# One decoder step on one core: mLSTM prompt tiles cut into chunk quarters, conv tails, a weight pair and token products moved

## What is computed

```
h = rmsnorm(x, norm_mix);  parts = split(h @ w_in)
h_a = mlstm_chunked(q, k, v, i, log_f, C0, n0, m0)      # chunks of 64 tokens, 4 heads of 128
h_b = gated_delta_chunked(conv(g_qkv), g, beta, S0)     # chunks of 64; conv over 4 tokens
h_c = memory_attention(x_q, mem_k, mem_v)               # 256 memory rows; 8 caches for the samples
mixed = sigmoid(gate_a)*(h_a @ w_a) + sigmoid(gate_b)*(h_b @ w_b) + sigmoid(gate_c)*(h_c @ w_c)
x = x + mixed @ w_out
x = x + hier_moe(rmsnorm(x, norm_ffn))                  # 16 experts of 512, best 2 of the best group
```

## Time and profile before

| what | value |
|---|---|
| median of three runs | 776.87 us (774.41 to 777.2) |
| the profiled execution | 773.82 us, its span 771.7 us, mean granted PE clock 0.98 |
| PE busy | 716.7 us (93%), 4393 records |
| DVE / ACT / POOL busy | 274.6 / 164.5 / 62.3 us |
| chain that ended last, by engine | PE 74%, DMA 15%, DVE 5%, ACT 2%, issue 2% |
| HBM | 174.43 MB read, 16.83 MB written |

### The profile page before, as it was taken

One profiled execution on the slowest core, in us unless ns is written; L12 is line 12 of the kernel. 1 busy time (PEld: TensorE's weight loads), 2 busy tenths in 40 slices (PEclk: granted clock), 3 DMA queues, 4 the chain that ended last, 5 costly groups with the idle time before them and its releaser, 6 DMA issues.

```text
span 771.7 us, 10609 instructions
## 1 busy us (share of the span) xinstructions
PE 716.7 (93%) x4393; PEld 422.0 (55%) x4393; DVE 274.6 (36%) x732; ACT 164.5 (21%) x377; POOL 62.3 (8%) x93
## 2 busy tenths in 40 slices
PE   6999999999989999999999999999999877878784
PEld 3544457877656777777777775543333323323331
DVE  1242013566763761464154352250232101100245
ACT  3221212222455411321131211231010000000014
POOL 3010200010330100000010020020000000001110
PEclk9999999999999999999999999999999989999998
DMA  9983700661399502023325487677999999999991
GB/s 271 343 284 109 192 27 1 236 252 72 96 393 371 187 6 106 1 84 138 109 73 214 138 278 315 243 314 259 391 424 427 407 429 430 411 425 398 431 358 64
DMA packets 49471, 187.25 MB, mean 243 GB/s; under 512 B 5240, under 2 KB 5485, under 8 KB 45322
## 3 DMA queue, kind: packets, MB, share of 16 engines
q1 hardware_dynamic: 40032, 155.52, 52.1%
q0 software_dynamic: 9280, 30.96, 12.1%
q10 hardware_dynamic: 106, 0.03, 0.0%
HBM read 174.43 MB, written 16.83 MB: 248 GB/s over the span
## 4 chain that ended last, share of the span: by engine, by line
PE 74%; DMA 15%; DVE 5%; ACT 2%; issue 2%; SPq 1%; POOL 1%; ACTq 0%; DVEq 0%
PE PS L664 13%; PE PS L1011 12%; DMA arena<-in_w_exp_down 9%; PE PS L1428 8%; PE PS L1023 6%; PE PS L1458 6%; PE PS L753 5%; DMA ring<-in_w_exp_down 3%; PE PS L675 2%; PE PS L780 2%; DMA out_C_s<-ring 2%; PE PS L650 2%; PE PS L1310 2%; PE PS L739 1%; SPq L1533 1%
## 5 line engine op out<-in xcount | busy, mean ns | idle before, releaser
L1428 PE MATMUL PS<-ring,arena 128*64 128x512 f32 x416 | 98.5, 629 | 13.7 <-issue 13.7
L1011 PE MATMUL PS<-hT,ring 128*128 128x288 f32 x384 | 102.2, 414 | 0.0
L1762 ACT ACTIVATE arena<-PS 128x512 f32<-128x512 f32 (+7 forms) x128 | 51.0, 422 | 183.5 <-PE PS L664 51.3
L1011 PEld LDWEIGHTS PS<-hT,ring 128*128 128x128 f32 x384 | 70.1, 190 | 19.6 <-issue 1.5
L1428 PEld LDWEIGHTS PS<-ring,arena 128*64 128x64 f32 x416 | 34.6, 144 | 73.0 <-issue 73.0
L664 PE MATMUL PS<-ring,hT 128*128 128x512 f32 x160 | 70.3, 596 | 0.0
L1762 ACT ACTIVATE brT<-PS 128x256 f32<-128x256 f32 (+4 forms) x37 | 15.6, 424 | 200.1 <-PE PS L1428 152.6
L1023 PE MATMUL PS<-brT,ring 128*128 128x288 f32 x192 | 50.5, 412 | 0.3 <-DVE arena L2557 0.3
L664 PEld LDWEIGHTS PS<-ring,hT 128*128 128x128 f32 x160 | 29.9, 190 | 37.3 <-issue 37.3
L753 PE MATMUL PS<-hT,ring 128*128 128x288 f32 x192 | 49.3, 410 | 0.9 <-DVE small L2325 0.9
L2968 DVE SCALAR_TENSOR_TENSOR brT<-brT,PS 128x256 f32<-128x256 f32 x16 | 6.7, 421 | 113.5 <-ACT brT L1762 113.5
(11 more groups left out here) (393 smaller groups left out, 866.9 us busy)
## 6 DMA issues: line engine op xcount, KB each, us to landing
ring<-in_w_in SPq DMA_DIRECT2D x15, 2048.0 KB, 10.3
ring<-in_w_exp_gate SPq DMA_DIRECT2D x13, 2048.0 KB, 23.9
ring<-in_w_exp_up SPq DMA_DIRECT2D x13, 2048.0 KB, 26.3
ring<-in_w_exp_down SPq DMA_DIRECT2D x8, 2048.0 KB, 26.0
arena<-in_w_exp_down SPq DMA_DIRECT2D x6, 2048.0 KB, 29.8
arena<-in_w_exp_gate SPq DMA_DIRECT2D x3, 2048.0 KB, 17.6
arena<-in_w_exp_up SPq DMA_DIRECT2D x3, 2048.0 KB, 22.4
moe_in<-in_table SPq DMA_DIRECT2D x2, 2048.0 KB, 23.8
```

The lines of the kernel that those rows point to most:

```text
L1011: ins = pe.matmul(PS[:, b, 0:T], w[:, 512 * k + 128 * (c % 4):512 * k + 128 * (c % 4) + 128], hT[:, k, :], start=(k == 0), stop=(k == KD - 1))
L1428: ins = pe.matmul(o[64 * hf:64 * hf + 64, :], hg[:, k, 64 * e:64 * e + 64], w[:, :, 512 * k + 256 * hf:512 * k + 256 * hf + 256], start=(k ...
L1762: return act.activation(o, i, f, **kw)
```

## The change

Six edits; nothing of what is computed changes, except in the order of sums.

1. Start: the memory norm vector has a tile of its own, `memrow`, loaded first and turned right behind memory tile 3; `vrow` without it is turned behind tile 4.
2. mLSTM tiles 0 and 1: `spread_rows` (the delta rule's too), `sc` and the intra-chunk `num` work on 64x64 quarters by `in_chunks`; the two halves off the diagonal are no longer written or read. `Cu` of both chunks is done in one go behind the first chunk's state part, chunk 0 in banks 1 and 2, chunk 1 in banks 0 and 3; DVE's second update waits for `num` too, whose multiplies read the old state.
3. Conv tails: turned in the routing (banks 0, 5, 4), copied and stored by ACT; POOL no longer waits for them, and DVE waits for the stores before it writes the first gathered rows over them.
4. `keep_busy` goes from four to three in front of the ranks and from three to one behind them. ACT copies keys 4 before `silu(0)`.
5. Pair 4 in halves: its first half is loaded when `gate_up(0)` has read half of its weights.
6. Last group: `to_tokens(0, 0)` and `to_samples(0)` stand before `gate_up(2)`, only `to_tokens(0, 1)` behind it, with banks and DVE's additions to match.

```diff
+        act.dma_start(memrow, a["mem_norm"][0].rearrange("(r c) -> r c", c=128)).then_inc(sg("mem_norm_in"), 16)
...
         def spread_rows(name, b, row, t):
-            for h in range(H):
-                ins = pe.matmul(o[0:n, h * n:(h + 1) * n], cst[0:H, C_SEL + 128 * h:C_SEL + 128 * h + n],
-                                row[:, t0:t0 + n], start=True, stop=True)
+            for h, r, hc in in_chunks(t):
+                ins = pe.matmul(o[r, hc], cst[0:H, C_SEL + 128 * h:C_SEL + 128 * h + m],
+                                row[:, t0 + r.start:t0 + r.stop], start=True, stop=True)
...
-            for h in range(H):
-                ins = pe.matmul(o[0:n, h * n:(h + 1) * n], kx[:, h * n:(h + 1) * n], qx[:, h * n:(h + 1) * n],
-                                start=True, stop=True)
+            for h, r, hc in in_chunks(t):
+                ins = pe.matmul(o[r, hc], kx[:, hc], qx[:, hc], start=True, stop=True)
...
-            for h in range(H) if t < 2 else ():
-                pe.matmul(oo[h // 2][0:n, (h % 2) * DA:(h % 2 + 1) * DA], sx[0:n, h * n:(h + 1) * n],
-                          v_a[0:n, t, h * DA:(h + 1) * DA], start=(h % 2 == 0), stop=False,
+            for h, r, hc in in_chunks(t) if t < 2 else ():
+                pe.matmul(oo[h // 2][r, (h % 2) * DA:(h % 2 + 1) * DA], sx[r, hc],
+                          v_a[r, t, h * DA:(h + 1) * DA], start=(h % 2 == 0), stop=False,
                           skip_group_check=True)
...
+                    if c == 0:
+                        uu = [[use(("Cu", t, 0, g), 1 + g), use(("Cu", t, 1, g), 3 * g)] for g in range(2)]
+                    for h in range(H) if c == 0 else ():
+                        for cc in range(2):
+                            rr = slice(L * cc, L * cc + L)
+                            ins = pe.matmul(uu[h // 2][cc][:, (h % 2) * DA:(h % 2 + 1) * DA],
+                                            k_t[rr, t, 128 * h:128 * h + 128], v_a[rr, t, h * DA:(h + 1) * DA],
...
+        pe.wait_ge(sg("tailT"), 1)
+        for g in range(3):
+            b = (0, 5, 4)[g]
+            o = use(("tail", g), b)
...
-        keep_busy(4)
+        keep_busy(3)
...
-        keep_busy(3)
+        keep_busy(1)
...
             down(0, p, g)
+            to_tokens(0, 0, p)
+            to_samples(0, p)
             gate_up(2, p, g)
-            to_samples(0, p)
-            to_tokens(0, 0, p)
             to_tokens(0, 1, p)
...
+            if first and q == NPAIR:
+                sp.wait_ge(sg("half_read"), 1)
+                for ex in range(2):
+                    sp.dma_start(dst[:, 0:2, :], src[:, 0:2, :]).then_inc(sg("d_first"), 16)
+                sp.wait_ge(*last_reader(0, p))
+                for ex in range(2):
+                    sp.dma_start(dst[:, 2:4, :], src[:, 2:4, :]).then_inc(ring_full[gslot("d", ex, 0)], 16)
+                return
...
+        for g in range(3):
+            copy_out(("tail", g), tails[:, 512 * g:512 * g + 512], bank_of(("tail", g))[0:HIST * (NB + 1), :])
+        act.wait_ge(*taken(("tail", 2)))
+        act.dma_start(out["conv_p"][0, 0], tails[0:HIST, :]).then_inc(sg("tail_out"), 16)
+        act.dma_start(out["conv_s"][0].rearrange("b s c -> (b s) c"), tails[HIST:, :]).then_inc(sg("tail_out"), 16)
...
+                    if c:
+                        dve.wait_ge(*filled(("num", t, g)))
...
+                if isinstance(p, int):
+                    dve.wait_ge(sg("tail_out"), 32)
                 slots_out(0, p, 0)
```

More of the change, by code:

```diff
@@ L250, in build @@
     wg, p = place(p, 128, KD, 16)
-    vrow, p = place(p, NV, 128)
+    vrow, p = place(p, NV - KD, 128)
+    memrow, p = place(p, KD, 128)
     crow, p = place(p, NB * HIST + CW, CCH)
@@ L290, in build @@
     qwm, _ = place(M0 + NB * DA, 128, H, NB, NS)
-    tails, _ = place(M0 + 4 * W, HIST * (NB + 1), CCH)
+    tails, _ = place(M0, HIST * (NB + 1), CCH)
     mixed, p = place(B0, 128, KD, T)
@@ L889, in _ @@
                             ins.then_inc(full[4 + h // 2], 1)
[L890 to L896 removed]
+                    if c == 0:
[5 more added lines that the diff above has]
+                                            k_t[rr, t, 128 * h:128 * h + 128], v_a[rr, t, h * DA:(h + 1) * DA],
+                                            start=(h % 2 == 0), stop=(h % 2 == 1), skip_group_check=True)
+                            if h % 2:
+                                ins.then_inc(full[uses[("Cu", t, cc, h // 2)][0]], 1)
                     fill_at(t, 2 + c)
@@ L963, in _ @@
         read_memory(1)
-        pe.wait_ge(sg("tailT"), 1)
-        for g in range(3):
-            b = (0, 5, 6)[g]
-            o = use(("tail", g), b)
-            for c in range(4):
-                ins = pe.transpose(o[0:HIST * (NB + 1), 128 * c:128 * c + 128], tailT[:, 4 * g + c, :], ident)
-            ins.then_inc(full[b], 1)
         def turn_sample_probabilities():
@@ L1067, in states_out @@
                           start=True, stop=True).then_inc(full[b], 1)
-        def in_chunks(t):
-            n, m = TILES[t][1], min(L, TILES[t][1])
-            return [(h, slice(c, c + m), slice(h * n + c, h * n + c + m)) for h in range(H) for c in range(0, n, m)]
         def turn_out(t):
@@ L1188, in _ @@
                 hp = [slice(NS * h, NS * h + NS) for h in range(H)]
-                for h in range(H):
-                    pe.wait_ge(sg(f"Ss_in{h}"), 16)
+                pe.wait_ge(sg("Ss_in"), 16 * H)
                 pe.wait_ge(sg("qdm"), 1)
@@ L1283, in _ @@
         logits(1).then_inc(full[1], 1)
-        keep_busy(4)
+        pe.wait_ge(sg("tailT"), 1)
+        for g in range(3):
+            b = (0, 5, 4)[g]
+            o = use(("tail", g), b)
+            for c in range(4):
+                ins = pe.transpose(o[0:HIST * (NB + 1), 128 * c:128 * c + 128], tailT[:, 4 * g + c, :], ident)
+            ins.then_inc(full[b], 1)
+        keep_busy(3)
         pe.wait_ge(sg("msk"), 1)
@@ L1430, in gate_up @@
                                     start=(k == 0), stop=(k == KD - 1))
+                if (g, e, k) == (0, 0, KD // 2 - 1) and isinstance(p, int):
+                    ins.then_inc(sg("half_read"), 1)
             ins.then_inc(gfull("gu", e), 1)
@@ L1451, in down @@
                         pe.wait_ge(*gready("d", 2 * pr_ + x, p, g))
+                    if (g, pr_) == (0, 0) and isinstance(p, int):
+                        pe.wait_ge(sg("d_first"), 32)
                 pe.wait_ge(*gtaken("dn", 2 * pr_ + nn, p, g))
@@ L1657, in _ @@
             value_rows(b)
-        pool.wait_ge(*taken(("tail", 2)))
-        pool.dma_start(out["conv_p"][0, 0], tails[0:HIST, :]).then_inc(sg("tail_out"), 16)
-        pool.dma_start(out["conv_s"][0].rearrange("b s c -> (b s) c"), tails[HIST:, :]).then_inc(sg("tail_out"), 16)
         pool.wait_ge(*filled("hcs"))
@@ L1968, in _ @@
         rows_out("gout", 2, gout, 1.0)
-        act.wait_ge(sg("Cp_out"), 16)
-        for g in range(3):
-            copy_out(("tail", g), tails[:, 512 * g:512 * g + 512], bank_of(("tail", g))[0:HIST * (NB + 1), :])
         gate_out(1)
@@ L2217, in mark @@
             dve.memset(scrap[:, marks[0]:marks[0] + 1], 0.0).then_inc(sem_, n)
-        dve.wait_ge(*filled("vec"))
-        cp(vecT, bank_of("vec")[:, 0:NV]).then_inc(freed("vec"), 1)
-        dve.wait_ge(*taken("vec"))
+        dve.wait_ge(*filled("memvec"))
+        cp(vecT[:, V_MEM:V_MEM + KD], bank_of("memvec")[:, 0:KD]).then_inc(freed("memvec"), 1)
+        dve.wait_ge(*taken("memvec"))
         for j in (3, 4, 0, 1, 2):
@@ L2224, in _ @@
             if j == 0:
+                dve.wait_ge(*filled("vec"))
+                cp(vecT[:, 0:NV - KD], bank_of("vec")[:, 0:NV - KD]).then_inc(freed("vec"), 1)
+                dve.wait_ge(*taken("vec"))
                 for i, (_, m) in enumerate(TILES):
@@ L2982, in group @@
                     add_rows(0, p, step)
+                    add_tokens(0, 0, 0, p)
+                    add_tokens(0, 0, 1, p)
+                    add_samples(0, p)
                 if (e, g) == (2, G - 1):
-                    add_samples(0, p)
-                    for nn in range(2):
-                        for t in range(2):
-                            add_tokens(0, nn, t, p)
+                    add_tokens(0, 1, 0, p)
+                    add_tokens(0, 1, 1, p)
                     add_rows(1, p, step)
```

41 lines of the change are left out of this document (21 added, 20 removed).

## The result

The changed kernel takes 768.62 us (median of 4 runs, 767.02 to 769.32), the kernel before on the same chip 777.04 (4 runs, 774.41 to 779.03): ratio 0.990, 95% interval 0.988 to 0.992, **8.4 us faster**. The forecast was a gain of 10.2. The profiled execution took 768.86 with a span of 767.0, where that of before took 773.82 and 771.7: by profiles only 5.0 are gained. So the question is where 2 to 5 us went. One difference between the kernels is not in the list of edits: PE waits for one semaphore on the samples' delta states (`Ss_in`) where it waited for four at the same place.

What follows compares the result with a forecast made beforehand. PE was taken to bound the kernel until pair 5's issue near 540 us, the weight stream after. Terms 1.4 + 2.0 + 0.7 + 2.2 + 1.1 + 1.6 + 1.2 = 10.2 gave 776.9 - 10.2 = 766.7 us, range 763.0 to 772.0.

Steps and rivals of the forecast that it cites:

- What bounds: Whole kernel: PE's work bounds it until about 540 us, when pair 5 is issued; the expert stage's weight stream after.
- Start 1.4: Program start: memory vector turned behind memory tile 3, so DVE and kvK start earlier; gain 1.4 us, bounds 0.7 to 1.4.
- mLSTM tile 0's spread "counts nothing": Spread row of mLSTM tile 0: shorter, but no gain, as PE waits 0.9 us behind it for a DVE copy.
- Spread rows 2.0: mLSTM tile 1 and both delta-rule tiles: eight 64-column multiplies replace four; gains 0.54, 0.94, 0.54; bounds 0 to 2.4 us.
- Scores 0.7: mLSTM scores on quarters: 0.89 us becomes 0.54 in each of two tiles; gain 0.7, bounds 0 to 0.7.
- `num` 0: Intra-chunk num: eight multiplies on two quarters overlap and again take 0.90 us; gain 0, bounds 0 to 2.3 lost.
- The rival in series (2.3): Intra-chunk num: quarters sharing a bank don't overlap, 2.3 us lost, total 769.0, or 771.2 if Cu fails too; chance 0.15.
- `Cu` 2.2: mLSTM Cu: both chunks' multiplies alternate on row halves and overlap, saving one 1.09 us group per tile; bounds 0 to 2.2.
- Keys 1.1: Keys 4 copied before silu(0): ACT's work after the landing is 1.1 us shorter; gain 1.1, bounds 0.5 to 1.9.
- Tails 0, `keep_busy` 1.6: Conv tails moved into the routing cost 0; fewer keep-busy multiplies behind the ranks let pick_rows start 1.6 us earlier.
- Last group 1.2: Expert stage's end: token products moved before gate_up(2); gain 1.2 us until the stream binds again, bounds 1.2 to 3.2.
- The clock: Rival in the routing: clock drops to 1.2 GHz behind the ranks until pair 5's issue, 26 us more, 793; chance 0.03.

Runs made afterwards that it cites:

- start_only: The kernel before with only the start edit (memory norm weights loaded and transposed on their own, DVE's copy of the other vectors later): 775.38 us, ratio 1.000.
- the second measurement: The changed kernel run once more, unedited, against the kernel before on the same chip: median 767.07 us, ratio 0.988.

## Why the prediction was right, and which steps failed

The direction, the range (763.0 to 772.0) and the chance of faster were right; 768.6 is 1.9 above the forecast 766.7. A part of this closeness is luck. The forecast added to the profile's scale the 3.1 by which the first three runs of before lay above its profile. Those runs were long ones: the medians of 11 to 17 further runs are 774.2 to 775.4. In the change the median lies 0.2 below the profile. On the profile's own scale 763.6 was forecast and 768.86 came, 5.3 more. Step by step:

- **What bounds.** Right, though the DMA row stands at 9 in slices 11 and 12 too, where PE wasn't held up. PE's chain sets the time up to pair 5, the stream from there. What PE is early with is handed over nearly whole (4.99 at pair 5, 5.31 at the issue of the last down weights' second halves).
- **Start 1.4.** kvK began 1.66 earlier in this pair of profiles, 1.2 in the mean. But alone it showed no gain (start_only), and the profiles with it have falls that the two without it haven't: the sum took a shift of the whole program as free.
- **mLSTM tile 0's spread "counts nothing".** It gave nothing, as said, and what stood behind the wait was no longer what the earlier trace rows show: fill(0) took 5.81.
- **Spread rows 2.0.** 0.47, 1.03 and 0.5: right, with the 1.03 owed to ACT's copies.
- **Scores 0.7.** This step failed: it was 0. The price came from the groups' own lengths; the groups on either side took the difference.
- **`num` 0.** 0.1 lost over two tiles. The rival in series (2.3) is out: L880 takes 1.04 until the next group, eight in series would take 2.06. The Trainium skill ("TensorEngine Tiling (Array Packing)", Restrictions and Gotchas) has it that different row tiles cannot access one PSUM bank at the same time. These two quarters write one bank, and the trace does not agree: the measurement decides.
- **`Cu` 2.2.** Right: 1.09 a tile.
- **Keys 1.1.** 1.0: the number is right, the reason only in part. PE's wait for ACT fell by 1.46, and 0.5 came back, 0.25 of it as a wait for cached keys to land, which the prediction didn't have.
- **Tails 0, `keep_busy` 1.6.** 0 and 1.47. The hole at L983 came as forecast (1.73) and cost nothing; `pick_rows` began 0.15 behind its matrix (506.53 + 0.56).
- **Pair 4 in halves 0.** Right. **Last group 1.2.** 0.7 in this pair of profiles, 0.5 in the mean of all; that the stream is the bound there was right.
- **Left out of the sum:** two falls of the clock, 3.4 together in the profiled execution. That, 0.7 for scores and 0.5 for `num`, keys, `keep_busy` and gate_up(0)'s wait, less 0.6 more at the start, is the 4.0 between the 9.0 forecast at pair 5 and the 4.99 there. For the medians this is not shown. They hold the scatter of both kernels besides: in the second measurement they are 774.22 and 767.07, 7.1 apart, with runs of the change from 763.15 up. How many executions have the falls is not known, and kvK alone ends anywhere between 24.0 and 26.4 in the twelve profiles with the start edit. The clock stood among the rivals, but in the routing, as an all-or-nothing loss of 26; it was full there, and fell at 116 and 489, where the prediction named no danger. Of the other rivals none came: in the profile of the change PE waits for DVE in the mLSTM tiles only ahead of fill(0), and DVE does not wait for the tails' stores.

What stays open: what decides whether a thin stretch costs the clock. Waits of 0.84 and 1.86 passed, one of 0.85 passed in the kernel before and not in two others, one of 2.04 did not, and at 488 PE did not wait at all (32x32 transposes and multiplies of 20 columns stand ahead). Open too is the end: from the last store's issue to the end of the span it takes 4.9 to 5.0 in the twelve profiles with the start edit, start_only among them, and 4.0 in the two without. The 6.8 and 6.1 in the expectations take the issue's start in the span off the whole time, which is 1.8 to 2.1 longer than the span. No run told why.

## What to carry to other kernels

Price a smaller shape from the start of one group to the start of the next but one, not by the group's own length: for the scores the neighbours took back all of the gain, for the spread row they took nothing. When a change moves everything earlier, look at the thin stretches again (waits of a microsecond, runs of short multiplies), since the clock may fall where it didn't, and one multiply put into a wait that is there anyway may keep it up. Where PE has less to do and another engine's copies stand behind it, take both as one term: the shorter spread row gave nothing until the copies were gone. And compare several profiles: one execution had the falls and others may not.

## What the hardware showed that was not expected

- The granted clock fell inside fill(0), while PE was busy (116.00 to 120.00: PE busy 4.00, granted clock 0.57), and cost 1.7 us each time: in the six profiles (of five kernels) that have the start edit and an unfilled wait of 0.85 or more ahead of it, in none of the six where the wait was filled or shortened, in neither of the two without the start edit. The second fall, in the out projection, followed in all six of the first kind, and in two of the second.
- Neither the length of the wait nor the time since the start decides alone. The eight multiplies of the out projection kept the clock when they began at 482.4, 485.2, 485.4, 489.0, 492.9 and 493.1, and lost it when they began at 483.6, 486.1, from 487.2 to 488.0, and at 494.9.
- kvK, the first long group, takes 14.0 to 16.6 us from profile to profile. In the change its first five records take 4.53, where at the upper level 16 records of this shape take 7.1. So the clock is at its lower level at the start, and when it rises differs. The granted clock in the windows doesn't show it: it reads 1.00 there, so this is read from the lengths of the multiplies.

```profile
9.00:14.00 5.00, 4.40 (x7) 1.98 (x7) 0.97 (x3) 0.00 (x0) 0.00 (x0) 1.00 1.02 283
```

- The same scores in halves of the array's columns (128 rows by 64 columns) cost about 0.3 around the group, 0.09 ahead of it and 0.2 in the eight multiplies behind, which is all that they gained; the spread row on 4 rows by 64 columns cost its neighbours nothing.
- Eight multiplies of 129 columns on two 64x64 quarters that write one PSUM bank took 1.04, where eight in a row would take 2.06: they ran side by side.
